# Ring places loaded singly, and the first expert's tokens gathered ahead of LN2

## The reference

```python
h = layer_norm(DEEPNORM_ALPHA * h + mix, ln1_g[l], ln1_b[l])
xatt = memory_cross_attention(h, mem_n, w_mem_q[l], w_mem_kv[l], w_mem_o[l])
h = layer_norm(DEEPNORM_ALPHA * h + xatt, ln2_g[l], ln2_b[l])      # "LN2"
ffn = moe_ffn(h, ...)
h = layer_norm(DEEPNORM_ALPHA * h + ffn, ln3_g[l], ln3_b[l])

def moe_ffn(h, w_router, b_router, w_mlp1, b_mlp1, w_mlp2, b_mlp2):
    logits = (xt @ w_router + b_router).astype(jnp.float32)
    top_val, top_idx = lax.top_k(logits, TOP_K)                     # 4 of 32
    top_w = jax.nn.softmax(top_val, axis=-1)
    ...
    for e in range(N_EXPERTS):                                      # w_mlp1[e] 1024x2048, w_mlp2[e] 1024x1024
        hid = clamped_swiglu(xt @ w_mlp1[e] + b_mlp1[e])
        y = y + combine[:, e:e + 1] * (hid @ w_mlp2[e] + b_mlp2[e])
```

## Time and profile before

| | us |
|---|---|
| times of three runs | 1141.17, 1142.33, 2108.56 |
| median | 1142.33 |
| span of the profiled execution, first to last instruction | 1139.4 |
| PE busy | 1088.4 (96%) |
| DVE busy | 320.1 (28%) |
| ACT busy | 224.3 (20%) |
| moved by DMA | 446.72 MB, mean 392 GB/s |

### The profile page before, as it was taken

One profiled execution on the slowest core, in us unless ns is written; L12 is line 12 of the kernel. 1 busy time (PEld: TensorE's weight loads), 2 busy tenths in 40 slices (PEclk: granted clock), 3 DMA queues, 4 the chain that ended last, 5 costly groups with the idle time before them and its releaser, 6 DMA issues.

```text
span 1139.4 us, 15654 instructions
## 1 busy us (share of the span) xinstructions
PE 1088.4 (96%) x6516; PEld 522.4 (46%) x6517; DVE 320.1 (28%) x723; ACT 224.3 (20%) x403; POOL 9.1 (1%) x14
## 2 busy tenths in 40 slices
PE   7999999999999999999999999999999999999996
PEld 6888899844333333334333333333333333334321
DVE  6887775562111111111211111111111101012113
ACT  5566565431000001001100000000000001001001
POOL 0000000000000000000000000000000000000000
PEclk9999999989999999999999999999999999999999
DMA  9766867599999999999999999999999999999995
GB/s 358 275 201 229 280 226 259 229 404 430 433 438 426 439 428 437 431 434 436 429 438 428 438 427 439 427 439 429 436 433 433 436 429 437 427 430 430 429 428 247
DMA packets 39967, 446.72 MB, mean 392 GB/s; under 512 B 4480, under 2 KB 5120, under 8 KB 24096
## 3 DMA queue, kind: packets, MB, share of 16 engines
q1 hardware_dynamic: 39936, 446.27, 93.6%
HBM read 445.21 MB, written 1.05 MB: 392 GB/s over the span
## 4 chain that ended last, share of the span: by engine, by line
PE 60%; DMA 36%; DVE 2%; SPq 1%; ACT 1%; issue 0%; DVEq 0%
DMA ring<-in_w_mlp 36%; PE bank L1025 24%; PE bank L1063 9%; PE bank L619 5%; PE bank L621 5%; PE bank L620 5%; PE bank L947 4%; PE bank L935 2%; PE bank L984 1%; PE bank L839 1%; PE bank L823 1%; PE bank L999 1%; SPq L452 1%; DMA live<-in_x_cols 0%; PE bank L606 0%
## 5 line engine op out<-in xcount | busy, mean ns | idle before, releaser
L1025 PE MATMUL bank<-ring,live 128*64 128x512 f32 x2048 | 472.9, 610 | 25.6 <-DMA ring<-in_w_mlp 25.0
L1025 PEld LDWEIGHTS bank<-ring,live 128*64 128x64 f32 x2048 | 144.7, 139 | 311.9 <-issue 293.2
L1063 PE MATMUL bank<-ring,live 128*64 128x512 f32 x992 | 220.3, 596 | 4.3 <-DMA ring<-in_w_mlp 4.3
L1743 DVE COPY live<-bank 128x256 f32<-128x256 f32 x32 | 13.6, 425 | 525.6 <-PE bank L977 525.6
L1063 PEld LDWEIGHTS bank<-ring,live 128*64 128x64 f32 x992 | 68.2, 137 | 130.1 <-issue 121.8
L1357 ACT ACTIVATE live<-bank 128x512 f32<-128x512 f32 x31 | 18.5, 597 | 324.4 <-PE bank L984 324.4
L1827 DVE TENSOR_SCALAR live<-bank 128x256 f32<-128x256 f32 x64 | 24.2, 420 | 198.9 <-PE bank L1025 198.9
L1429 DVE TENSOR_TENSOR w_low<-w_raw,w_high 128x1024 fp32r<-128x1024 f32 x63 | 74.5, 1221 | 15.4 <-ACT w_high L1152 14.9
L619 PE MATMUL bank<-w_high,left 128*128 128x512 f32 x160 | 64.4, 402 | 7.2 <-DVE w_low L1599 7.1
L1152 ACT ACTIVATE w_high<-w_raw 128x1024 fp32r<-128x1024 f32 x63 | 64.7, 1063 | 27.9 <-DMA w_raw<-in_w_in 12.7
L1353 ACT ACTIVATE live<-live 128x512 f32<-128x512 f32 x32 | 20.3, 635 | 246.1 <-DVE live L1827 246.1
(11 more groups left out here) (224 smaller groups left out, 788.3 us busy)
## 6 DMA issues: line engine op xcount, KB each, us to landing
ring<-in_w_mlp SPq DMA_DIRECT2D x73, 4096.0 KB, 46.9
ring<-in_w_mlp SPq DMA_DIRECT2D x42, 2048.0 KB, 48.3
w_raw<-in_w_in SPq DMA_DIRECT2D x23, 512.0 KB, 8.8
w_raw<-in_w_mem_kv SPq DMA_DIRECT2D x16, 512.0 KB, 5.0
ring<-in_w_mlp SPq DMA_DIRECT2D x8, 1024.0 KB, 37.5
w_raw<-in_w_mix_out SPq DMA_DIRECT2D x8, 512.0 KB, 5.6
w_raw<-in_w_mem_q SPq DMA_DIRECT2D x8, 512.0 KB, 3.8
w_raw<-in_w_mem_o SPq DMA_DIRECT2D x8, 512.0 KB, 5.1
```

What stands on the lines that cost most here:

```text
L1025: mm = pe.matmul(up[j][64 * g:64 * g + SLOTS, :], x_e[:, k, :], columns(row, j, g), start=False, stop=(k == KC - 1))
L1063: mm = pe.matmul(to[64 * g:64 * g + SLOTS, :], stationary[:, P * c + 64 * u:P * c + 64 * u + SLOTS], slot(at)[:, col:col + 512], start=(u ...
```

## The change

Six edits, which all lie between about 180 and 300 us of the span.

1. **Places.** `prefetch` takes one place or two. After unit 59 is issued, place 10 alone; after the last unit the order is 11, 22+23, 14+15, 18, 16, 19, 12+13, 17, 20, each behind the wait of its own tile. Place 21 (under `gb`) comes later, amid expert 2's loads. Expert 2's first two places are loaded singly too, behind `first_used` (k = 0) and `up_used` 1 (k = 1). The transfer of `b2` moves from ahead of expert 2 to behind its first slots. A new transfer brings 8 KB, `token_cols` (LN2's gain and bias as columns).
2. **ACT** copies `h` to `h2` and the tables ahead of its last four splits, not behind them.
3. **Centred sums.** ACT subtracts the mean from `h2` (`centre`), one instruction for each token tile, once `rT` is copied. DVE's `centre` and `stretch` are gone from between the logits.
4. **Gather.** `pick_first` holds 1/deviation in place of one. `gather_first` multiplies the centred sums (as weights of 128 columns) by `pick_first` (64 columns), so the tokens come out turned; it stands behind both ranks. `turn_first` and the copies to and from `first_rows` are gone.
5. **Gain and bias** of LN2 are applied as `x_e` is copied out of PSUM, one instruction for each k: ACT the even, DVE the odd.
6. **LN2 itself** (`normalise`, eight DVE instructions) follows after that, and `h_part`/`take_part` after it. DVE reads the number of sweeps before it waits for the last parts.

```diff
+            def centre(t):
+                act.wait_ge(minus_ready, t + 1)
+                act.activation(h2[:, t, :], h2[:, t, :], ACT.Identity, bias=small[:, 6 + t:7 + t]).then_inc(centred, 1)
...
             def gather_first(t):
-                for i in range(2):
-                    for q in range(2):
-                        at = 512 * q + S * i
-                        mm = pe.matmul(banks[3 + 4 * i][64 * q:64 * q + SLOTS, 0:S], pick_first[:, t, :], h2[:, t, at:at + S],
-                                       start=(t == 0), stop=(t == 1))
+                for c in range(KC):
+                    at = 4 * P * (c // 4) + c % 4
+                    mm = pe.matmul(first_tokens(c), h2[:, t, at:at + 4 * P - 3:4], pick_first[:, t, :],
+                                   start=(t == 0 and c < 2), stop=(t == 1 and c >= KC - 2), skip_group_check=True)
...
+            for c in range(0, KC, 2):
+                act.activation(x_e[:, c, :], first_tokens(c), ACT.Identity, bias=token_cols[:, 1, c:c + 1],
+                               scale=token_cols[:, 0, c:c + 1]).then_inc(x_even if c < KC - 2 else x_e_ready, 1)
...
-            prefetch([10, 22, 14, 18, 12, 16, 20])
+                if u == 59:
+                    prefetch(10, 1)
+            prefetch(11, 1)
+            prefetch(22)
+            prefetch(14)
+            prefetch(18, 1)
+            prefetch(16, 1)
+            prefetch(19, 1)
+            prefetch(12)
+            prefetch(17, 1)
+            prefetch(20, 1)
+            for quarter, used, landed in ((0, first_used, third_in), (1, up_used, first_half_in[0])):
+                sp.wait_ge(used, 1)
+                part = slice(2048 * quarter, 2048 * (quarter + 1))
+                sp.dma_start(slot(0)[:, part], expert_src(2, 0)[:, part]).then_inc(landed, 16)
+            sp.wait_ge(up_used, 2)
+            load_half(2, 0, 0, 1)
+            prefetch(21, 1)
...
+                elif place in (14, 18):
+                    wait_unit_used(sp, 59)
+                elif place in (16, 19):
+                    wait_unit_used(sp, 61)
+                elif place in (12, 17, 20):
+                    wait_unit_used(sp, 63)
+                elif place == 21:
+                    sp.wait_ge(ln_ready, 12)
```

More of the change, by code:

```diff
@@ L482, in load_down_halves, with prefetch @@
                 load_half(e, UPS, 3 * parity + UPS, 1)
[L484 to L488, removed]
+            def prefetch(place, count=2):
+                free_places(place)
+                part = slice(2048 * (place % 4), 2048 * (place % 4 + count))
+                sp.dma_start(slot(place // 4)[:, part], expert_src(place // 12, place % 12 // 4)[:, part])\
+                    .then_inc(early_in[place // 2], 16)
             for u in range(RAW, UNITS * len(BLOCKS)):
@@ L989, in columns, with wait_early, up_stage @@
                 return rows[:, 1024 * j:1024 * (j + 1)].rearrange("p (m a n) -> p m a n", a=2, n=8)[:, :, g, :]
-            def up_stage(n, at, loads, first_loads=None, earlier=None, first=False, first_sum=False, weights=False, bias=False, tokens=False, scatter_first=False):
+            def wait_early(half):
+                pe.wait_ge(early_in[half], 16 * EARLY_LOADS[half])
+            def up_stage(n, at, loads=None, first_loads=None, earlier=None, first=False, first_sum=False, weights=False, bias=False,
+                         tokens=False, scatter_first=False, early=False, quarter_in=None):
                 pe.wait_ge(hot_ready, n)
@@ L1028, in up_stage @@
                         mm.then_inc(up_used if k < KC - 1 else up_done, 1)
+                    elif first and k == 0:
+                        mm.then_inc(first_used, 1)
                     if k == 1 and earlier is not None and earlier[0] is not None and not scatter_first:
@@ L1046, in gather_next, with down_stage @@
                 gather()
-            def down_stage(n, at, loads, to, first_loads=None, stationary=hidT, between=None, halves=(None, None)):
+            def down_stage(n, at, loads, to, first_loads=None, stationary=hidT, between=None, halves=(None, None), early=False):
                 pe.wait_ge(hidT_ready, n)
@@ L1116, in scatter_before @@
                 scatter()
-            down_stage(of_end[0], downs[1], loads, up[1], 64, last_hidT, between=scatter_before, halves=last_half_in)
+            down_stage(of_end[0], downs[1], loads, up[1], 48, last_hidT, between=scatter_before, halves=last_half_in)
             pe.wait_ge(y_ready, of_end[0])
@@ L1332, in take_tokens @@
                 act.activation(x_e[:, :, :], banks[3][:, :].rearrange("p (c n) -> p c n", c=KC), ACT.Copy).then_inc(x_e_ready, 1)
-            h_part(0, 0)
-            act.wait_ge(first_summed, 1)
-            act.activation(first_rows[:, 0:S], banks[3][:, 0:S], ACT.Copy).then_inc(first_low_half, 1)
-            act.wait_ge(gathered, 1)
-            for q in range(2):
-                act.activation(x_e[:, 4 * q:4 * q + 4, :], banks[3][:, :].rearrange("p (c a n) -> p a c n", c=4, a=2)[:, q, :, :],
-                               ACT.Copy).then_inc(x_e_ready if q else x_half_ready, 1)
             act.wait_ge(best_ready, 1)
```

205 lines of the change are left out of this document (105 added, 100 removed).

## The result

The changed kernel takes 1145.79 us (median of seven runs, 1143.93 to 1147.02) against 1142.08 for the kernel before, measured again beside it. The ratio is 1.0035, with a 95% interval of 1.0025 to 1.0044: 2.9 to 5.0 us slower. Forecast were 1143.8 us and a loss of 1.5. The profiled run took 1144.67 us with a span of 1142.9, so 1.8 us lie around the span and not the 2.9 of the prediction, which had set one run's span against the median of others; the profiled run before is the one of 1141.17, also 1.8 over its span.

A forecast was written before the change was run, and what follows sets the result against it. The DMA queue was taken as the bound: a 4.6 us lead would be given back in a dry stretch with 1.5 us more, so 1139.4 + 1.5 of span plus 2.9 around it made 1143.8 us, range 1138.5 to 1147.5.

The forecast's parts named there:

- The bound: Whole kernel: the DMA queue sets the end; other engines' times count only where they delay or hasten a load.
- Part 1, the issues: Places ahead of the experts: issues at 181, 206.5, about 210 and 217.5 us, filling the dry stretches.
- Part 1, "the queue is 4.6 us ahead": Loads ahead of the experts: 13 places landed at 243.4 us instead of 248.0, the most the change can give.
- Part 2, the gather: First expert's gather on PE: 32 passes at twice 0.115 us, 7.3 us in all, ending at 243.1 us.
- The rival of the quick gather: First expert's gather: passes stay near 0.115 us, gather ends at 239.5, span 1140.2 us; chance 0.30.
- Part 2, the releases: First up stage: starts near 243.9 us, k = 0 done at 247.0, k = 1 at 248.9; queue dry 243.4 to 249.4.
- Part 2, the loads after it: Expert 2's places: land at 251.8 and 254.2 us, with 22 places there at 271.9 against 270.4 before.
- Part 3: LN2 and routing parts behind the tokens: ready at 260.4 us, PE waits about 1 us, nothing lost, 3 us reserve.
- The sum: Whole kernel: 1139.4 + 1.5 = 1140.9 us of span, with 2.9 us around it 1143.8 against 1142.33.
- Single places: Ten loads of one place: 424 GB/s against 435 for pairs, 0.06 us each, nothing worth a term.

The follow-up runs named there:

- e4: Changed kernel plus eight unused wide products, four ahead of each rank, to hold the clock up; ratio 1.0035 to the kernel before.
- r1: Changed kernel with the first expert's tokens gathered in rows from the centred sums, then turned; LN2 still later; ratio 1.0001 to the kernel before.
- e1: Kernel before with single places, `b2` behind expert 2's loads and ACT's copies ahead of its splits; old gather and LN2; ratio 1.0001.
- e3: Changed kernel with only one of token tile 1's gather products made, so the first expert gets tile 0's tokens; ratio 1.0000 to the kernel before.
- b1: Changed kernel with only the `b2` transfer moved back ahead of expert 2's loads; ratio 1.0025 to the kernel before.
- e5: Changed kernel with the first expert's gather reading 128 neighbouring columns as weights instead of every fourth; ratio 1.0033 to the kernel before.
- e6: Kernel before with single places and ACT's earlier copies, old gather and LN2, `b2` ahead of expert 2's loads; ratio 0.9995.
- f2: Kernel before with single places, ACT's earlier copies, 9 wide products in PE's pauses and `b2` ahead of expert 2's loads; ratio 0.9980, median 1139.47 us.
- g1: Changed kernel with row gather, seven wide products in PE's pauses, `b2` ahead of expert 2's loads, place 21 asked for sooner; ratio 0.9983, median 1139.81 us.

## Why the prediction was right in direction and short in size

The time fell in the range and on the side of the forecast, at 1145.8 for 1143.8. By its own steps:

- **The bound** was right. All but 0.6 us of the difference between the spans is there when 32 places have landed.
- **Part 1, the issues** came as forecast with the 1.2 us taken off: place 10 at 180.1, 11 at 205.4, 22 at 208.6 (forecast 209.7), the last three between 229.5 and 230.3. The two dry stretches filled as the earlier trace rows against the rows above show.
- **Part 1, "the queue is 4.6 us ahead"** is the term that failed, and with it the 1.5 us. The schedule put 13 places at 243.4; with this run's 1.2 us taken off that is 242.2, and they landed at 244.2. The data had come on time, though: the 2 us from 242 show 33 GB/s at a DMA share of 0.08, which of 16 engines is one still at work while 15 have finished. A load counts when its slowest engine is done: this one landed as the last bytes came, and from 244 to 246 us nothing was moved. The landings of before that I started from had this lag in them, and the schedule for after had none. By landings on both sides the lead was 248.0 - 245.4 = 2.6 us. By bytes it was less. What was moved from 199 us on, before and after:

```profile
199.00:244.86 45.86, 43.08 (x217) 33.17 (x217) 27.25 (x75) 16.61 (x29) 2.09 (x2) 0.89 0.73 295
199.00:242.30 43.30, 41.49 (x214) 36.43 (x213) 17.92 (x49) 14.93 (x24) 1.10 (x2) 0.92 0.74 291
```

Before, that is 13.5 MB or 12.9 places, with 12 landed, so the 13 were moved by 245.1 and not by 248.0. After, it is 12.0 places, and place 10 was there already: 13 by 242.3, or 243.5 with the 1.2 us. The lead was some 2 us and not 4.6.

- **Part 2, the gather** was forecast at 7.3 us and took 7.70. The size was nearly right and the reason half wrong: I doubled the logits' pass for the low clock, but the stride of four costs as much at the full clock (e4). The first step came 0.8 us after the gather's end, as my 243.1 and 243.9 have it, though the 1.06 us that I named for it would give 244.2. The rival of the quick gather, at 0.30, was dead for that reason too, whatever the clock did.
- **Part 2, the releases** fit: k = 0 used 3.1 us after the stage's start (forecast 3.1), k = 1 4.8 (5.0), and 6.0 us dry, from 242.4 to 248.4. The stage started at 243.4, which with the 1.2 us is 0.7 later than forecast.
- **Part 2, the loads after it** landed later than scheduled. The first landed at 251.2 and the second at 254.6, where the schedule less 1.2 gives 250.6 and 253.0, and 22 places were there at 273.7 (`b2` just behind them), where 271.6 less 1.2 was forecast; before, they were there at 270.8 for 270.4. The last seven took 273.7 - 254.6 = 19.1 us, where seven at 2.42 are 16.9. Half of these 2.2 us is the lag, which the dry stretch had wiped out and which came back; the landings of before carried it from the start. The other half is flow: the queue moved 408 GB/s in them, where the kernel before moved 431 in the last 14.9 us of its own count, and most of that is missing where `b2` crosses.
- **Part 3** held: LN2 was over at 249.4 (forecast 250.5), `gather(1)` began at 258.87 after a wait of 0.44 us, and r1 shows no cost of LN2's place.
- **The sum**: 1.5 us were forecast, and 4.1 are there once the early front part is taken off (3.7 by the medians). The forecast was a loss of 6.1 us against a lead of 4.6; what came is a loss of about 6 against a lead of about 2. So the lead was sized wrong, since it was counted with the lag on one side and without it on the other. The loss came out near its size, and that was in part luck, since terms were left out on both sides: the 0.7 us of the later stage and the up to 0.8 of `b2` against the some 0.7 us that the kernel before lost itself from 248 to 250 us (217 and 340 GB/s).
- **Single places** ran at 425 GB/s in the last stage, and e1, which has ten of them, is at 1.0001: as the prediction held. The Trainium skill, "DMA: Bandwidth & Descriptors", section "Bandwidth", gives 341 GB/s for a transfer of 1 MB, and these traces go on disagreeing with it as long as other loads are queued.

## What to carry to other kernels

Where a queue feeds from what an engine frees, filling it sooner is worth little if the next release stays where it was (e1: 3.5 us ahead at 24 places, and 1.0001); look first at when that release comes. In r1 and e3 the stage began 2.3 and 3.3 us sooner after the gather's start, and each took back some 3.5 us. A small transfer among big ones can cost more than its bytes; issue it where the queue stands dry (b1). When a gather or transpose is rewritten, count its weight loads, not its products: 32 loads of 128 strided float32 columns cost 7.7 us where 16 loads of 64 columns, with wide data moved past them, cost 3.7. A schedule of loads made from landings has the slowest DMA engine in it; make the one for the changed kernel the same way.

## What was not expected of the hardware

- **A strided float32 weight load costs the same at both clocks**: 0.24 us for 128 columns with a stride of four (e4, 1.00 for 9 passes and 0.50), against 0.115 packed at 1.00 and 0.22 packed at 0.50 (e5).
- **One of 16 DMA engines falls behind.** In the kernel after all but some 66 KB of the queue's data was there at 242 us, and place 20 landed 2.2 us later. The lag is lost when the queue runs dry and grows again under load (about 1.1 us over 7 places there). What makes it grow is open: no run here tells the candidates apart, of which the fetching of instructions by DMA is one (24 packets in the profile's page of the kernel after).
- **A transfer of 128 KB on 32 partitions costs more than its bytes** among others: 0.4 to 0.8 us of flow, seen in every trace with `b2` behind expert 2's loads and in none with it ahead (from 264 to 276 us). Why is open.
- **The clock's way back differs.** After its fall to 0.50 (1.2 GHz) it came back after 10.2 us in the kernels before and after, 13.65 in e1 and 6.8 in e6 with the same PE program, 13.65 in b1 with the PE program of the kernel after, and 3.4 in f2 and g1. With wide products in the pauses it was 3.4 to 6.8 us in four of five runs; in the fifth, e4, the clock fell later, amid the strided gather, and stayed low for 10.2. With one profile each, the part of chance is open.
